# Latent up-projections as jobs of the closing block, gate tiles on another queue

## The reference

```
cq, ckv, kr, z = split(h @ w_in, [384, 640, 672])
q  = (rmsnorm(cq)  * g_q ) @ w_uq    # 16 heads x (64 plain + 32 rotated)
kv = (rmsnorm(ckv) * g_kv) @ w_ukv   # 16 heads x (64 keys + 64 values)
k_rope = rope(kr)                    # 32 wide, shared by all heads
o = softmax(mask((q_nope.k_nope + q_rope.k_rope) * 96**-0.5)) @ v;  out = o * silu(z)
```

## Time and profile before

| what | us |
|---|---|
| median of 3 runs | 3240.16 (3235.9 to 3241.09) |
| profiled execution, its own time | 3234.05 |
| its span | 3232.2 |
| TensorE busy | 2960.0 (92%) |
| VectorE, ScalarE, GpSimd busy | 1913.8, 1575.7, 1244.5 |
| granted TensorE clock, mean | 0.959 |

### The profile page before, as it was taken

One profiled execution on the slowest core, in us unless ns is written; L12 is line 12 of the kernel. 1 busy time (PEld: TensorE's weight loads), 2 busy tenths in 40 slices (PEclk: granted clock), 3 DMA queues, 4 the chain that ended last, 5 costly groups with the idle time before them and its releaser, 6 DMA issues. The chain is left out here.

```text
span 3232.2 us, 40805 instructions
## 1 busy us (share of the span) xinstructions
PE 2960.0 (92%) x13514; PEld 2324.8 (72%) x13536; DVE 1913.8 (59%) x2771; ACT 1575.7 (49%) x2778; POOL 1244.5 (39%) x1044
## 2 busy tenths in 40 slices
PE   8999977778899999999677789999999999799998
PEld 6888875555688778888565467777777777578877
DVE  3544215444278774444555568778787787347875
ACT  3111114556444544444223167777777777544553
POOL 0022002223132541000210068888888888523353
PEclk9999988889899999999898789999999999899999
DMA  5255349664897665554567924252442522399764
GB/s 176 72 125 124 106 107 190 155 156 117 274 295 242 234 231 195 177 173 147 191 261 289 293 62 105 69 125 69 95 103 69 125 69 53 100 301 284 235 222 159
DMA packets 268849, 531.15 MB, mean 164 GB/s; under 512 B 46376, under 2 KB 94632, under 8 KB 260080
## 3 DMA queue, kind: packets, MB, share of 16 engines
q1 hardware_dynamic: 215696, 412.78, 44.5%
q10 hardware_dynamic: 52960, 116.02, 11.5%
HBM read 351.06 MB, written 177.37 MB: 163 GB/s over the span
## 5 line engine op out<-in xcount | busy, mean ns | idle before, releaser
L2161 POOL TENSOR_TENSOR mla_pl<-mla_p,mla_ph 128x512 fp32r<-128x512 f32 (+3 forms) x640 | 707.2, 1120 | 361.0 <-ACT mla_p L2023 352.5
L1324 PE MATMUL end_bank<-end_xh,end_whi 128*128 128x512 f32 x1600 | 633.1, 396 | 49.9 <-DVE end_xl L1510 28.7
L1325 PE MATMUL end_bank<-end_xl,end_whi 128*128 128x512 f32 x1600 | 625.0, 391 | 0.0
L1326 PE MATMUL end_bank<-end_xh,end_wlo 128*128 128x512 f32 x1600 | 625.0, 391 | 0.0
L1881 PE MATMUL mla_score<-mla_q,mla_k 96*128 96x512 f32 (+7 forms) x1920 | 555.7, 392 | 6.3 <-DMA mla_q<-mla_m_t 6.3
L1496 DVE TENSOR_TENSOR end_wlo<-end_wraw,end_whi 128x1024 fp32r<-128x1024 f32 x188 | 256.4, 1364 | 366.7 <-ACT end_whi L1379 366.2
L1379 ACT CAST end_whi<-end_wraw 128x1024 fp32r<-128x1024 f32 x188 | 197.2, 1049 | 552.8 <-PE end_bank L1326 516.2
L2022 ACT ACTIVATE mla_ph<-mla_score 128x512 fp32r<-128x512 f32 (+3 forms) x640 | 341.0, 533 | 225.8 <-PE mla_score L1881 222.8
L1881 PEld LDWEIGHTS mla_score<-mla_q,mla_k 96*128 96x128 f32 (+1 forms) x1920 | 362.8, 193 | 91.5 <-issue 36.8
L2053 DVE TENSOR_REDUCE mla_mx<-mla_mx 128x1 f32<-128x512 f32 (+3 forms) x640 | 371.9, 603 | 94.2 <-PE mla_mx L1881 93.6
L2099 DVE TENSOR_TENSOR mla_acc<-mla_acc,mla_p 128x512 f32<-128x512 f32 (+3 forms) x576 | 348.6, 605 | 118.6 <-ACT mla_p L2023 114.6
(11 more groups left out here) (233 smaller groups left out, 4695.7 us busy)
## 6 DMA issues: line engine op xcount, KB each, us to landing
end_wraw<-in_w_out ACTq DMA_DIRECT2D x64, 512.0 KB, 7.8
end_wraw<-in_pe_gate ACTq DMA_DIRECT2D x64, 512.0 KB, 4.8
end_wraw<-in_w_in ACTq DMA_DIRECT2D x56, 512.0 KB, 3.8
swa_q<-scratch_q_hi SPq DMA_DIRECT2D x32, 512.0 KB, 9.3
end_raw<-scratch_o SPq DMA_DIRECT2D x32, 512.0 KB, 11.7
end_factor<-scratch_inv SPq DMA_DIRECT2D x64, 256.0 KB, 10.0
scratch_proj<-end_out_f SPq DMA_DIRECT2D x64, 256.0 KB, 7.0
scratch_sum<-end_out_f SPq DMA_DIRECT2D x64, 256.0 KB, 6.5
```

What stands on the lines that cost most here:

```text
L1324: nc.tensor.matmul(bank, wh[:, at], xh[:, k0 + k, :], start=(k == 0), stop=False)
L1325: nc.tensor.matmul(bank, wh[:, at], xl[:, k0 + k, :], start=False, stop=False)
L1326: last = nc.tensor.matmul(bank, wl[:, at], xh[:, k0 + k, :], start=False, stop=(k == kc - 1))
L2161: pool.tensor_tensor(p_lo[b][:, off:TC], prob[b][:, off:TC], p_hi[b][:, off:TC].bitcast(F32), ALU.subtract).then_inc(p_lo_ok, 1)
```

## The change

- In both attention phases gate tiles are loaded by ScalarE's queue. In the windowed one there are five gate buffers and the load is issued two chunks ahead; in the latent one three, issued at the chunk's first step.
- In the windowed attention all low parts are GpSimd's.
- The phases "uq" and "ukv" are gone. The closing block of layer 0 has eight more jobs: four "uq" (12 tiles of 3 row blocks, six weight blocks of two tiles) and four "ukv" (8 key tiles and 8 value tiles of 2 row blocks, four weight blocks). Their weights are loaded once for each quarter of the tokens. Low parts of these weights are GpSimd's, and so are the scaling by the norm and the sums of the rotation.
- The sums of squares, which the products with ones put on all partitions, are turned into factors where they stand (`rms_means`, `rms_roots`, `rms_inverse`): no row is stored and read back.
- The shared key is rotated at the end of each "in" job (its tile is now the last); the sums of squares are folded one tile earlier.
- Values are stored per block of 128 tokens, in pieces of 512 bytes.

```diff
-            jobs += [("in", q) for q in range(NTC)]
+            jobs += [(stage, q) for stage in ("in", "uq", "ukv") for q in range(NTC)]
...
+            elif stage == "uq":
+                for pair in (0, 3, 1, 4, 2, 5):
+                    b = new_block(stage, pair, 2, 2 * Q_LORA)
+                    turning = pair in (1, 2)
+                    for i in range(2):
+                        tiles.append(dict(job=j, kind="turn" if turning else "split", q=q, block=b, at=i, ...
+            elif stage == "ukv":
+                for g in range(2):
+                    b = new_block("uk", g, 2, KD * P)
+                    tiles += [dict(job=j, kind="split", i=4 * g + i, q=q, block=b, at=i) for i in range(4)]
+                for h in range(2):
+                    b = new_block("uv", h, 1, KD * P)
+                    tiles += [dict(job=j, kind="v", i=h, q=q, block=b, at=i) for i in range(4)]
...
+                if kind == "split":
+                    sp.dma_start(dst[0][x["i"], :, tok(q)], out_f[place[n]][:]).then_inc(stored[place[n]], 16)
+                    sp.dma_start(dst[1][x["i"], :, tok(q)], out_l[place[n]]).then_inc(stored[place[n]], 16)
+                elif kind == "v":
+                    sp.dma_start(latent["v"][x["i"] * 8:(x["i"] + 1) * 8, :, 4 * q + x["at"], :].rearrange(
+                        "h p d -> p h d"), v_tile(n).rearrange("p h two d -> p h (two d)")
+                        ).then_inc(v_stored[values[n] % 3], 16)
...
+                elif x["kind"] == "split":
+                    act.wait_ge(product, n + 1)
+                    wait_out_free(act, n)
+                    act.copy(out_f[place[n]][:].bitcast(F32R), bank).then_inc(hi_ok, 1)
+                elif x["kind"] == "v":
+                    act.wait_ge(product, n + 1)
+                    wait_v_free(act, n)
+                    act.copy(v_tile(n)[:, :, 0, :].bitcast(F32R), bank...).then_inc(hi_ok, 1)
...
+            def rms_means(q):
+                dve.wait_ge(stat_ok, NTC + q + 1)
+                vec.tensor_scalar(var[:], stat_ps[0][:], 1.0 / Q_LORA, RMS_EPS, ALU.mult, ALU.add)
+                vec.tensor_scalar(mean_sq[:], stat_ps[1][:], 1.0 / KV_LORA, RMS_EPS, ALU.mult, ALU.add
+                                  ).then_inc(rms_var, 1)
+            def rms_inverse(q):
+                dve.wait_ge(rms_root, q + 1)
+                vec.reciprocal(rstd[q][:], var[:])
+                vec.reciprocal(mean[q][:], mean_sq[:]).then_inc(rms_ok, 1)
...
+            def split_w(b):      # GpSimd, blocks of uq, uk, uv
+                pool.wait_ge(w_hi_ok, b + 1)
+                pool.tensor_tensor(w_lo[b % n_w][:, 0:width], w_raw..., w_hi..., ALU.subtract).then_inc(w_lo_p_ok, 1)
+            def rms_x(n):
+                for k in range(part_of(n).start, part_of(n).stop):
+                    op = pool.tensor_tensor(raw[j % 2][:, k, :], raw[j % 2][:, k, :], norm_of[stage][q][:], ALU.mult)
+            def turn_sums(n):
+                pool.tensor_tensor(old[0][:], old[0][:], old[1][:], ALU.subtract).then_inc(turn_sum, 1)
+                pool.tensor_tensor(old[2][:], old[2][:], old[3][:], ALU.add).then_inc(turn_sum, 1)
...
-        small = 3
+        small, n_gate = 3, 3 if long else 5
...
-            for c in range(len(chunks)):
-                u = chunks[c][0]
-                if c + 1 < len(chunks):
-                    load_gate(c + 1)
+            def load_gate(c):                       # now ScalarE
+                if c >= n_gate:
+                    act.wait_ge(gated, c - n_gate + 1)
+                act.dma_start(cfg["gate"](gate[c % n_gate]), cfg["gate_src"](*chunks[c])
+                              ).then_inc(gate_in[c % n_gate], 16)
+            ahead = n_gate - 3
...
+                    if st["first"] and c and c + ahead < len(chunks):
+                        load_gate(c + ahead)
                     act.wait_ge(scores, g + 1)
...
-                    if on_vector(g):
-                        low_part(g)
...
-                if g < total and not on_vector(g):
+                if g < total:
```

More of the change, by code:

```diff
@@ L1065, in chain_phase @@
+                    tiles.append(dict(job=j, kind=kind, i=i, q=q, block=b, at=0))
         total = len(tiles)
         first.append(total)
[L1067 to L1076, removed]
+        block_end = [b["at"] for b in blocks[1:]] + [total]
@@ new lines, in chain_phase, with upto @@
+        w_upto = [16 * sum(blocks[c]["loads"] for c in range(b % n_raw, b + 1, n_raw)) for b in range(len(blocks))]
+        n_dve_blocks = sum(b["stage"] not in ("uq", "uk", "uv") for b in blocks)
+        def upto(*kinds):
+            counts, n = [], 0
+            for x in tiles:
+                n += x["kind"] in kinds
+                counts.append(n)
+            return counts
+        by_act, by_dve = upto("proj", "lat"), upto("wo", "pe", "z", "split", "v", "turn", "kr")
+        outs, olds, turns = upto("pe"), upto("wo", "pe"), upto("pe", "z")
@@ L1078, in row_of @@
+        highs, rotated, values = upto("split", "v"), upto("turn", "kr"), upto("v")
         def row_of(x):
             return latent["rows"][x["i"]] if x["kind"] == "lat" else 0 if x["kind"] == "wo" else None
-        for n, x in enumerate(tiles):
-            squares.append(sum(row_of(y) is not None for y in tiles[:n + 1]))
+        squares = [sum(row_of(y) is not None for y in tiles[:n + 1]) for n in range(total)]
         old_tiles = [n for n, x in enumerate(tiles) if x["kind"] in ("wo", "pe")]
-        wo_upto = [sum(y["kind"] == "wo" for y in tiles[:n + 1]) for n in range(total)]
+        wo_upto = upto("wo")
@@ L1087, in row_ends @@
+        v_tiles = [n for n, x in enumerate(tiles) if x["kind"] == "v"]
         def row_ends(n):
@@ L1735, in attention_phase @@
         den_row = [s.sb(f"den_row{b}", [1, TC]) for b in range(small)]
-        gate = [s.sb(f"gate{b}", [HEAD_DIM, TC]) for b in range(small)]
+        gate = [s.sb(f"gate{b}", [HEAD_DIM, TC]) for b in range(n_gate)]
         o_out = [s.sb(f"o_out{b}", [HEAD_DIM, TC]) for b in range(small)]
@@ L1816, in at_slot @@
             return mine[k] if k < len(mine) and u + 1 < units else []
-        def on_vector(g):
-            return not long and not flat[g][2]["last"]
-        low_at = [[], []]
-        for g in range(total):
-            low_at[on_vector(g)].append(g)
-        low_count = [low_at[on_vector(g)].index(g) + 1 for g in range(total)]
         tail = store_lag + 1
@@ L2325, in close_layer @@
                 gain=a[f"ln_g{layer}"], bias=a[f"ln_b{layer}"], latent=latent))
-        def rms(name, sums, gain):
-            factors = dram(name, [1, SEQ])
-            return dict(kind="rms", cols=SEQ // P, sources=[spread(sums)], folded=[spread(factors)], order=[2],
-                        rows=factors, gain=gain, eps=RMS_EPS)
         q0, k0 = parts("q0", [2, KV_HEADS, P, SEQ]), parts("k0", [2, 1, P, SEQ])
```

499 lines of the change are left out of this document (356 added, 143 removed).

## The result

The changed kernel takes 3189.88 us (median of 4 runs, 3187.74 to 3194.12) against 3239.58 us (4 runs) of the kernel before: ratio 0.985 [0.9835, 0.9866], 50 us less. The forecast was 3178 us; the direction and the range hold, the time is 12 us above. The two profiled executions stand at 3190.66 and 3234.05 us, 43.4 us apart, and the trace splits that into three pieces. From the start to the first product of the first closing block: -25.7 us (820.3 to 794.6). From there to the first product of the latent attention: -15.3 us (1010.6 to 995.3). The rest: -2.4 us.

The account below looks back on a forecast made before the run. Elsewhere TensorE-bound; time to gain lay in the windowed attention's gate waits and the up-projections' gaps. 3234.05 - 52 - 10 = 3172 us, given as 3178 because the median is 6 us higher; own range 3155 to 3203, with rivals 3118 to 3222.

Parts of the forecast that it names:

- Part 1: Windowed attention: gate tiles on ScalarE's queue, two chunks ahead, end the wait behind bulk loads; 53 us saved, bounds 25 to 65.
- I take 32 us per unit: Windowed attention: units 1 to 5 fall from 42.6 us to 32, three above the better limit of products and transfers.
- Rival B: Windowed attention: gate wait becomes a wait for keys and values; units of 37.6 us, 25 us saved, 3206 us; chance 0.15.
- Rival C: Windowed attention: queues interleave without gain, by the skill's rule; only the up-projection change is left, 3230 us; chance 0.04.
- Part 2: Windowed attention: all low parts on GpSimd set no new bound; later hand-over in the last unit costs 1 us (0 to 9).
- Part 3: Up-projections as closing-block jobs: two starts go, transfers bound the jobs; 273.4 us against 283.7, -10 us, bounds -74 to +34.
- delay in the input jobs: Closing block: two reciprocals in one VectorE tile make the next weights' low part about 2 us late each; 6 us (0 to 10).
- four query jobs: Closing block: transfers of 9.96 MB per job at 372 GB/s take 26.8 us each, longer than the products' 24.5 us.
- four key/value jobs: Closing block: transfers take 34.7 us per job, 18.3 at 372 GB/s and 16.4 for value stores at 256 GB/s.
- Rival A: Up-projection jobs: the transfers hide and products are the bound; 64 us less than forecast, 3114 us; chance 0.12.
- Rivals D and F: Up-projection jobs: D moves at 298 GB/s, 3223 us; F, an order on one engine, would look like D; joint chance 0.13.
- Rival E: Up-projection jobs: TensorE, waiting for stores in every tile, is held at 1.2 GHz; 3301 us, slower than before; chance 0.04.

Follow-up runs that it names:

- experiment 1: Kernel before with gate tiles on ScalarE's queue (five buffers, two chunks ahead), low parts still split; 3221.75 us, ratio 0.9954.
- experiment 9: Kernel before with gate tiles kept on SyncE's queue but asked for seven chunks ahead (nine gate buffers); 3200.86 us, ratio 0.9881.
- experiment 2: Kernel before with all low parts of the windowed attention on GpSimd, gates left in place; 3232.95 us, ratio 0.998.
- 3: Changed kernel with the attention phases of the kernel before, so only the up-projections as jobs remain; 3219.84 us, ratio 0.9947.
- experiment 4: Changed kernel with six output and denominator row buffers in the windowed attention instead of three; 3162.74 us, ratio 0.9768.
- the best version: Changed kernel with six output buffers, values in pieces of 4 KB and the reciprocals in two tiles; 3141.42 us, ratio 0.9703.
- 10: The best version with low parts of the windowed attention split again between VectorE and GpSimd, as in the kernel before; 3153.95 us, ratio 0.974.
- experiment 6: Changed kernel with the two reciprocals of the root-mean-square factors in two tiles instead of one; 3181.76 us, ratio 0.9821.
- 8: Changed kernel with up-projection weights loaded for the first quarter of the tokens only; 3168.7 us, ratio 0.9785.
- Experiment 5: Changed kernel with latent values laid out by token, so stores write pieces of 4 KB instead of 512 bytes; 3180.18 us, ratio 0.9816.

## Why the prediction was right, and where it was off

**Part 1, the wait for the gate goes: right.** It is gone in every version that orders the gates ahead (experiments 1, 9), and stays where they aren't (49.1 us in 2, 50.0 in 3).

**"I take 32 us per unit": the step that failed.** What was weighed as late next was the transfers, and they do fit: with the stores out of the way a unit takes 30.8 us, unit 2 at a share of 1.00, as the sum "29 to 30 us of full use" had it. The wait for the gate was worth 5 x 11.8 = 59 us, between the 53 taken and the upper bound of 65. Some of that is the clock: 0.88 in unit 2 before, 1.00 in experiment 4. What the list of late things lacked was on ScalarE's queue itself. The prediction counted the 64 issues there at 0.62 us and gave them 0, nearly right, but did not say what a gate load waits for (`gated` of an earlier chunk), nor what stands behind that wait (the exponentials), nor that the stores in the same queue free only three output buffers. Of the two, the stand of ScalarE seems to weigh more: experiment 9 is without it and 22 us faster than 1, at nearly the same wait for stores. Before, single stores took up to 15.0 us too, and the late gate hid them (VectorE waited 5.5 us for them in all). Price: 27 us (experiment 4, the denominators' buffers included). The windowed attention brought 25.7 us instead of 52, also because its first exponential starts 3.7 us later (509.63 against 505.94), which was not traced to a cause. It is on time where the gates stay in their old place (0.0 and 0.9 us late in experiments 2 and 3) and 1.3 to 4.5 us late in every version that moves them, 9 among them (2.2).

**Rival B gave the unit's time, not the mechanism.** It had units of 37.6 us, and 37.0 were measured; but it expected a wait for keys and values, and none is in the rows. Its number must not be taken as evidence for it.

**Rival C, the rule of the queues, is out, but no second queue was needed.** C had nothing for part 1; in experiment 1 the gate wait of 49.9 us is gone, and 16.6 us with it. Experiment 9 takes 39 us without any second queue, and the changed kernel's second queue added a conflict of its own. The Trainium skill, page "DMA: Bandwidth & Descriptors", section "Issuing engines are not separate DMA queues", has it that spreading transfers saves issue time only. The case agrees in so far as the larger gain came without another queue. It does not agree that nothing comes earlier, though in experiment 1 queue, lead (two chunks) and buffers (five) changed together, and no run moves the queue alone.

**Part 2, "cost 1 us": wrong in sign.** It is a gain: 5.4 us alone (experiment 2), 12.5 us in the best version (10). GpSimd's longer instruction was priced at the end of a chain, and VectorE's relief at nothing, since it was idle half the time. The share of busy time misled there.

**Part 3, -10 us: right, by terms that were each a little off.** From the last input product to the latent attention 259.5 us, and 10.4 us more in the input jobs (322.0 against 311.6): 269.9 against the forecast's 273.4.

| term | forecast | measured |
|---|---|---|
| delay in the input jobs | 6 | 10.4 |
| four query jobs | 107.2 | 110.3 |
| four key/value jobs | 138.8 | 129.4 |
| tail | 21.4 | 19.8 |

The delay was called by its cause, three gaps behind the reciprocals (2.1 to 2.3 us each by the starts of the products); the rest of it went with them in experiment 6, among it two short falls of the clock. The query jobs are in the forecast's time: 110.3 us here, 105 to 107 in experiments 3, 4 and 6. That their weights' transfers lengthen them is shown by 8, where they run at the products' pace; bytes and landing time of the weights went together there and were not parted. The key/value jobs are bound by transfers too (8, and a share above 1), though not by them alone (5). Their term was too large: 129.4/4 = 32.4 us less 18.3 for the rest leaves 14.1 us for 4.19 MB, 297 GB/s and not 256. That is no constant: the same sum gives 28.7 - 12.7 = 16.0 us, 262 GB/s, in experiment 8, where fewer weights are loaded. Long pieces take 4.6 us off these jobs and 10 us off the kernel. The Trainium skill, page "DMA: Bandwidth & Descriptors", section "Specifications", gives 512 B as the least transfer for the full rate. Experiment 5 does not bear that out: in pieces of 4 KB the same bytes went at 346 GB/s and a share of 0.94 to 1.00, in pieces of 512 bytes at 330 and 1.01 to 1.03.

Of the signs named ahead, a DMA share above 0.9 and ScalarE waiting for stores of values came, and so did TensorE under 0.7 in the forecast's own measure (67%); the 77% of the rows is another measure, in which a product behind a gap or at the lower clock counts for more than 0.227 us (0.50 for the one at 1288.59).

**Rival A** (products bound part 3) is out: they are 87 of the 129.4 us of the key/value jobs. **Rivals D and F** (291 us for the eight jobs) too: 239.7 us. **Rival E**: the clock falls in single stretches (0.89 in the third query job, 0.91 in the second key/value job) and comes back; it is never held at 1.2 GHz.

**The errors partly cancelled.** On the profiled executions the forecast was -62 and -43.4 was measured: +26 us in the windowed attention, -5 us in part 3 and -2 us elsewhere. The offset of 6 us to the median held for the kernel before, not for the changed one, whose profiled execution lies 1 us above its median; hence 12 us on the medians. The windowed attention by itself missed the range given for it (52 +- 8, measured 25.7); that the kernel's time lies in the range is partly luck.

## What to carry to other kernels

When a load moves to another engine's queue, write down what its issue waits for and what stands behind it on that engine, and what else that queue carries: here the issue cost next to nothing by itself, but the wait ahead of it held the exponentials; three more output buffers took back 27 us. The wait that is removed hides the next one at the same instruction; look for every semaphore that this instruction waits on, not only for the one that came last before. When only one tile is late in a queue, try its place in the order first.

## What was not expected

- Moving subtractions to an engine that takes 1.78 times as long for each (1285 against 722 ns) made the kernel 5 to 12 us faster (experiments 2 and 10), with the slower engine busy 63% of a unit.
- Of the three gaps of 2 us on a TensorE that was otherwise full, the second and the third ended with a fall of the granted clock to 0.50 for 3.4 us, the first did not; without the gaps the clock was 1.00 for all 311.7 us. That the gaps cause the falls was not tried by itself. The stretches behind the first gap (it ends at 1288.59) and the second (1368.79):

```profile
1288.60:1292.00 3.40, 3.40 (x15) 2.82 (x16) 3.33 (x6) 0.00 (x0) 0.00 (x0) 1.00 0.70 203
...
1369.00:1372.00 3.00, 3.00 (x8) 2.32 (x9) 2.96 (x5) 0.00 (x0) 0.00 (x0) 0.50 0.71 191
```

- In the windowed attention a DMA share of 1.00 goes with 226 GB/s, in the key/value jobs one of 1.02 with 329 GB/s: here the share, not the rate, tells when the transfers are full.
